# Half tiles for a depthwise convolution, column groups for its norm's sums, and x loaded in pieces

## The reference, cut to what matters

```
u = h @ w_in + b_in                       # h: 2064 x 1024, w_in: 1024 x 3072
a, ga, z = split(u, 3)
glu = a * sigmoid(ga)
c = conv(glu, w_dw) + b_dw                # depthwise over time, 31 taps, causal
c = silu(layer_norm(c, norm_g, norm_b))   # over the 1024 channels
y = (c * silu(z)) @ w_out + b_out
h = layer_norm(ALPHA * h + y, g, b)
```

## Time and profile before

| | us |
|---|---|
| median of three runs (2564.4 to 2571.88) | 2570.7 |
| the profiled execution, its own time | 2562.57 |
| its span on the core | 2560.8 |
| TensorE busy | 2403.9 (94%) |
| VectorE busy | 1304.0 (51%) |
| ScalarE busy | 1099.3 (43%) |
| GpSimd busy | 847.4 (33%) |
| DMA, all queues | 134.50 MB, mean 53 GB/s |

### The profile page before, as it was taken

One profiled execution on the slowest core, in us unless ns is written; L12 is line 12 of the kernel. 1 busy time (PEld: TensorE's weight loads), 2 busy tenths in 40 slices (PEclk: granted clock), 3 DMA queues, 4 the chain that ended last, 5 costly groups with the idle time before them and its releaser, 6 DMA issues. The chain is left out here.

```text
span 2560.8 us, 33174 instructions
## 1 busy us (share of the span) xinstructions
PE 2403.9 (94%) x12822; PEld 1256.0 (49%) x12822; DVE 1304.0 (51%) x2013; ACT 1099.3 (43%) x2060; POOL 847.4 (33%) x592
## 2 busy tenths in 40 slices
PE   7999999868999799999999998997999997999898
PEld 3555555443444355555555554443655554443343
DVE  3898888987553333434334334776145443243422
ACT  5665555345663333434334334334255554222211
POOL 0788777555887101010101010442033332000000
PEclk9999999988999899999999999998999998999899
DMA  5011111032324100100100003223300000100332
GB/s 192 25 42 42 42 42 37 14 132 69 108 99 164 62 1 5 50 1 5 42 1 13 1 1 124 91 87 108 71 9 18 9 1 21 33 1 1 139 105 91
DMA packets 49853, 134.50 MB, mean 53 GB/s; under 512 B 5088, under 2 KB 19040, under 8 KB 48681
## 3 DMA queue, kind: packets, MB, share of 16 engines
q1 hardware_dynamic: 49704, 132.47, 15.5%
HBM read 96.65 MB, written 35.80 MB: 52 GB/s over the span
## 5 line engine op out<-in xcount | busy, mean ns | idle before, releaser
L390 DVE SCALAR_TENSOR_TENSOR cm_tap_sum<-cm_glu,cm_prm,cm_tap_sum 128x2048 f32<-128x2048 f32 x168 | 395.5, 2354 | 49.2 <-ACT cm_tap_sum L248 44.5
L317 POOL TENSOR_TENSOR mixed<-mixed,cm_tap_products 128x2048 f32<-128x2048 f32 x71 | 325.7, 4587 | 88.8 <-ACT cm_tap_products L269 72.7
L91 PE MATMUL cm_proj<-H_hi,cm_w_ga_hi 128*128 128x416 f16 (+1 forms) x640 | 217.8, 340 | 21.9 <-DVE H_lo L364 18.6
L92 PE MATMUL cm_proj<-H_lo,cm_w_ga_hi 128*128 128x416 f16 (+1 forms) x640 | 217.9, 340 | 0.0
L93 PE MATMUL cm_proj<-H_hi,cm_w_ga_lo 128*128 128x416 f16 (+1 forms) x640 | 217.7, 340 | 0.0
L91 PE MATMUL gm_vr<-gm_wvr_hi,H_hi 128*128 128x512 f16 (+1 forms) x544 | 202.8, 373 | 0.0
L93 PE MATMUL gm_vr<-gm_wvr_hi,H_lo 128*128 128x512 f16 (+1 forms) x544 | 202.8, 373 | 0.0
L92 PE MATMUL gm_vr<-gm_wvr_lo,H_hi 128*128 128x512 f16 (+1 forms) x544 | 202.8, 373 | 0.0
L1408 POOL TENSOR_TENSOR gm_q_inter<-gm_q_rel,gm_block_decays 128x512 f32<-128x512 f32 x16 | 16.8, 1047 | 467.0 <-ACT gm_block_decays L1487 467.0
L1943 POOL TENSOR_TENSOR at_probs<-at_probs,at_rsum 128x768 f32<-128x768 f32 (+1 forms) x64 | 90.4, 1412 | 179.1 <-DVE at_rsum L2186 178.9
L1762 DVE SCALAR_TENSOR_TENSOR gm_v_r<-gm_vr,gm_v_r 128x256 f32<-128x256 f32 x64 | 27.1, 424 | 236.9 <-ACT gm_v_r L1506 236.9
(11 more groups left out here) (361 smaller groups left out, 5583.2 us busy)
## 6 DMA issues: line engine op xcount, KB each, us to landing
cm_w_stage<-conv_w SPq DMA_DIRECT2D x24, 512.0 KB, 3.8
co_rows<-x_rows SPq DMA_DIRECT2D x16, 512.0 KB, 4.4
h_rows<-co_rows SPq DMA_DIRECT2D x16, 512.0 KB, 2.9
mixed<-gla_w SPq DMA_DIRECT2D x8, 1024.0 KB, 7.1
go_rows<-h_rows SPq DMA_DIRECT2D x16, 512.0 KB, 4.0
h_rows<-go_rows SPq DMA_DIRECT2D x16, 512.0 KB, 2.8
fo_rows<-h_rows SPq DMA_DIRECT2D x16, 512.0 KB, 3.6
out<-fo_rows SPq DMA_DIRECT2D x16, 512.0 KB, 2.6
```

The costliest lines, as they stand in the source:

```text
L91: nc.tensor.matmul(out, w_hi, x_hi, start=first, stop=False)
L92: nc.tensor.matmul(out, w_hi, x_lo, start=False, stop=False)
L317: nc.gpsimd.tensor_tensor(c_tile(j), c_tile(j), prod[:, r % 2, :], ALU.add).then_inc(s_add, 1)
L390: nc.vector.scalar_tensor_tensor(out=acc[:, :], in0=window(j, k), scalar=col(j, k), in1=acc[:, :], op0=ALU.mult, op1=ALU.add).then_inc(s_t ...
```

## The change

**conv_mix.** A tile is worked on in two halves of 1024 columns, 16 units U. Each half has its own half of the PSUM sum. A first half can start once three of the five token tiles have their glu. The first six units (channel tiles 0 to 2) have 8 products and 21 taps as before; the ten others have 9 products and 20 taps. The products have three slots of 1024 columns. VectorE's taps are no longer given in shares per tile but by `taps_due`. x comes in four pieces per token tile, each with its own semaphore, and the first sections wait piece by piece. The first three weight pieces are scaled inside the halving. `first_tokens` is made in four parts of two channel tiles, one per round 4 to 7.

**conv_out.** Each sum's 8 matmuls have a 128x32 matrix and write to four different 32-partition groups of the bank (k modulo 4), two in each. ScalarE copies both sums to SBUF, and one matmul each with a 128x128 matrix adds the four groups (`totals`), inside the next row. All 8 squares have their own room. The stages of groups 2, 3 and 4 move: totals, mean square and `finish` one row later, `NORMS` one row later, `UNITS` of group 2 in rows 2 to 4 as 3, 3, 2. SyncE's wait before row 3 goes; the ones matrix is set by VectorE.

```diff
@@ conv_mix: counts, schedules, ScalarE and, last, VectorE
-        ACT_TAPS, SUM_TAPS = 1, 9
-        BEFORE = (2, 4, 5, 5, 5)
+        HALF = SEQ // 2
+        UNITS = 2 * KT
-        prod = m.sb("tap_products", [P, 2, SEQ])
+        prod = m.sb("tap_products", [P, 3, HALF])
+        XP = 4
+        def n_products(U):
+            return 8 if U < 6 else 9
+        def taps_before(U):
+            return sum(TAPS - 2 - n_products(V) for V in range(U))
+        def taps_due(j, t):
+            if j < 2:
+                early = max(0, 2 + 6 * (NTT * j + t - 3))
+            else:
+                early = 45 + 9 * (NTT * (j - 2) + t)
+            U, more = ((2 * j - 1, 5), (2 * j - 1, 14), (2 * j - 1, 18), (2 * j, 7), (2 * j, 16))[t]
+            return min(early, taps_before(U) + more if U >= 0 else 0)
...
                 def load_x(t):
+                    for q in range(XP):
+                        sp.dma_start(x_piece(xs, t, q), x_piece(xT.rearrange("(k p) n -> p k n", p=P), t, q)).then_inc(s_x[t][q], 16)
...
+                def start_sum(U):
+                    act.wait_ge(s_glu, U // 2 * NTT + (NTT if U % 2 else 3))
+                    if U >= 2:
+                        act.wait_ge(s_ring, sum_slot(U - 2) + 1)
+                def products(U, first, last):
+                    for i in range(first, last + 1):
+                        r = slot(U, i)
+                        if r >= 3:
+                            act.wait_ge(s_add, r - 2)
+                        nc.scalar.activation(prod[:, r % 3, :], window(U, i), ACT.Copy, scale=col(U // 2, i)).then_inc(s_ring, 1)
+                def read_sum(U):
+                    r = sum_slot(U)
+                    act.wait_ge(s_tap, taps_before(U + 1))
+                    act.wait_ge(s_add, r - 2)
...
+                for j in range(KT):
+                    U = 2 * j
                     for t in range(NTT):
+                        if j and t == 0:
+                            if j >= 2:
+                                read_sum(U - 3)
+                            start_sum(U - 1)
+                            start_c(U - 1)
+                        gate(j, t)
+                        if j and t == 0:
+                            products(U - 2, 7, n_products(U - 2))
+                            products(U - 1, 1, 1)
+                        elif j and t == 1:
+                            products(U - 1, 2, 5)
+                        elif t == 2:
+                            if j:
+                                products(U - 1, 6, 6)
+                                read_sum(U - 2)
+                            start_sum(U)
+                            start_c(U)
+                            if j:
+                                products(U - 1, 7, n_products(U - 1))
+                        elif t == 3:
+                            products(U, 1, 3)
+                        elif t == 4:
+                            products(U, 4, 6)
...
+                for j in range(KT):
+                        taps(done, taps_due(j, t))
+                        done = max(done, taps_due(j, t))
+                        if j >= KT // 2 and t == 2:
+                            first_tokens(j - KT // 2)
+                        gated(j, t)
+                taps(done, taps_before(UNITS))
@@ conv_out
+        TOTALS = {s + 1: T for s, T in STATS.items()}
+        NORMS = {0: (1, range(KT)), 2: (2, range(4)), 3: (2, range(4, 8)), 5: (3, range(4)), 6: (3, range(4, 8)),
+                 9: (4, range(4)), 10: (4, range(4, 8))}
+        UNITS = {0: (1, range(KT)), 2: (2, range(3)), 3: (2, range(3, 6)), 4: (2, range(6, 8))}
+        CG = 4
+        def of_group(ap, k):
+            return ap[k % CG * (P // CG):(k % CG + 1) * (P // CG), :]
+                def group_sums(T):
...
                     for k in range(KT):
-                        nc.tensor.matmul(mean(T), ones[:, :], c_tile(T, k), start=(k == 0), stop=(k == KT - 1))
+                        mm = nc.tensor.matmul(of_group(mean(T), k), ones[:, :], c_tile(T, k), start=(k < CG), stop=(k >= CG))
...
+                def totals(T):
+                    pe.wait_ge(c_cp, 2 * T + 2)
+                    nc.tensor.matmul(mean(T), total[:, :], part[:, 0, 0:w], start=True, stop=True).then_inc(c_e2, 1)
+                    nc.tensor.matmul(spread_of(T), total[:, :], part[:, 1, 0:w], start=True, stop=True).then_inc(c_e2, 1)
```

More of the change, by code:

```diff
@@ L300, in _ @@
+                        if t == (0 if j else 2):
+                            split_w(j, Z)
+                        elif t - 1 in ((0, 1) if j else (2, 3)) and j + 1 < KT:
+                            split_w(j + 1, t - 1 if j else t - 3)
                         if j >= LAG:
                             silu_z(j - LAG, t)
+                read_sum(UNITS - 3)
+                start_sum(UNITS - 1)
+                start_c(UNITS - 1)
+                silu_z(KT - 2, 0)
+                products(UNITS - 2, 7, n_products(UNITS - 2))
@@ new lines, in _ @@
+                silu_z(KT - 2, 1)
+                read_sum(UNITS - 2)
+                products(UNITS - 1, 1, 1)
+                silu_z(KT - 2, 2)
+                products(UNITS - 1, 2, 3)
+                silu_z(KT - 2, 3)
+                products(UNITS - 1, 4, 5)
+                silu_z(KT - 2, 4)
+                products(UNITS - 1, 6, 7)
+                silu_z(KT - 1, 0)
+                products(UNITS - 1, 8, n_products(UNITS - 1))
+                for t in range(1, NTT):
+                    silu_z(KT - 1, t)
@@ L308, in keep_first, with add, add_products, add_sum @@
                     nc.gpsimd.tensor_copy(first[:, j, :], glu[:, j % 2, 0:HALO + META]).then_inc(s_first, 1)
-                def add(j, i):
-                    r = ring_before(j) + i
-                    if i == 0:
-                        pool.wait_ge(s_base, j + 1)
-                    else:
+                def add(U, r):
+                    if slot(U, 1) == r:
+                        pool.wait_ge(s_base, U + 1)
+                    if r:
                         pool.wait_ge(s_add, r)
                     pool.wait_ge(s_ring, r + 1)
-                    nc.gpsimd.tensor_tensor(c_tile(j), c_tile(j), prod[:, r % 2, :], ALU.add).then_inc(s_add, 1)
+                    nc.gpsimd.tensor_tensor(c_unit(U), c_unit(U), prod[:, r % 3, :], ALU.add).then_inc(s_add, 1)
+                def add_products(U, first, last):
+                    for i in range(first, last + 1):
+                        add(U, slot(U, i))
+                def add_sum(U):
+                    add(U, sum_slot(U))
                 def split_w(j, s):
@@ L380, in gated, with taps @@
                         in1=sig[:, i % 2, 0:w], op0=ALU.add, op1=ALU.mult).then_inc(s_glu, 1)
-                def taps(j, first_tap, n):
-                    for i in range(first_tap, first_tap + n):
+                def taps(first, last):
+                    for n in range(first, last):
+                        U = max(V for V in range(UNITS) if taps_before(V) <= n)
+                        i = n - taps_before(U)
                         if i == 0:
-                            dve.wait_ge(s_init, j + 1)
+                            dve.wait_ge(s_init, U + 1)
@@ L418, in _ @@
                 dve.wait_ge(s_ps, 3)
-                for j in range(KT + 1):
-                    done = 0
+                done = 0
+                for j in range(KT):
                     for t in range(NTT):
@@ L554, in conv_out @@
         ident = m.sb("ident", [P, P])
-        ones = m.sb("ones_over_d", [P, P])
+        ones = m.sb("ones_over_d", [P, P // CG])
+        total = m.sb("sum_of_groups", [P, P])
         prm = m.sb("norm_prm", [P, 2 * KT])
-        sq = m.sb("c_squares", [P, 2, GROUP])
+        part = m.sb("group_sums", [P, 2, GROUP])
         sl = m.sb("silu", [P, R, GROUP])
@@ L787, in _ @@
                     if s in STATS:
-                        square(STATS[s], 0)
-                        square(STATS[s], 1)
+                        squares(STATS[s], range(KT))
+                    if s in TOTALS:
+                        mean_square(TOTALS[s])
                     if s >= 2:
@@ L836, in transposes @@
                         mm.then_inc(s_tr, 1)
-                stats(0)
-                stats(1)
+                group_sums(0)
+                totals(0)
+                group_sums(1)
+                totals(1)
                 for s in range(NS + 2):
@@ L855, in _ @@
                             mm.then_inc(s_mm, 1)
+                            if s in TOTALS and h == 0:
+                                totals(TOTALS[s])
                     if s == 2:
@@ L892, in normed @@
                     scaled(ks[-1])
+                nc.vector.memset(ones[:, :], 1.0 / D).then_inc(s_ones, 1)
+                nc.vector.memset(total[:, :], CG / P).then_inc(s_ones, 1)
                 for i, e in enumerate((LN_EPS / ALPHA ** 2, LN_EPS)):
```

276 lines of the change are left out of this document (132 added, 144 removed).

## The result

The changed kernel takes 2536.9 us (median of 4 runs, 2535.0 to 2538.3), the kernel before beside it 2570.0 (4 runs): a ratio of 0.9874, 95% interval 0.9857 to 0.9892. It is faster, by a little over half of what I forecast. The profiled execution spans 2535.4 us, 25.4 less than the one of before.

| stretch | before | after | measured | forecast |
|---|---|---|---|---|
| conv_mix | 559.0 | 526.6 | -32.4 | -36 |
| start of conv_out, to row 1 | 64.0 | 59.9 | -4.1 | -8 |
| rows 1 to 12 | 163.5 | 161.8 | -1.7 | -13.5 |
| row 13 to the gate stage's first product | 62.1 | 64.7 | +2.6 | 0 |
| gate stage to the bias product of attention | 934.6 | 934.9 | +0.3 | 0 |

What follows compares the result with a forecast made beforehand. It took TensorE, with VectorE's waits and tail, to bound conv_mix, and TensorE, with GpSimd next, conv_out. 36 + 8 + 13.5 = 57.5 from 2562.6 gave 2505; with 2513 from the median it took 2509, range 2494 to 2537.

Steps and rivals of the forecast that it cites:

- conv_mix, 36 us forecast: conv_mix: the stage, with its last VectorE add at 520, ends near 523 us instead of 559.
- four banks give it 12 us of room, so I count nothing for it: conv_mix: ScalarE's `gate` stands behind products waiting for slots; counted as 0, or 0 to 8 us without the room.
- the 48 us of GpSimd's work in 42: conv_mix, round 1: GpSimd has 18 adds and three weight halves, 48.4 us in 42; round 2 takes the 6 back.
- the sign that I had named for being wrong: GpSimd as releaser of TensorE's waits, named beside a conv_mix end past 535 us.
- my second rival: GpSimd's ring sets the pace, ScalarE held behind full slots, row 5 later: 8 + 6 us, 2523 in all; 14%.
- the 4 us that I gave for the lower clock and late pieces: conv_mix start: allowance added to the first matmul at 7.7 and 501 us of matmuls, so TensorE alone ends at 513.
- Start of conv_out, 8 us forecast: conv_out before row 1: row 1 starts 56 us into the stage instead of 64.
- About 2.8 us earlier through the chain to `normed` of group 1: Start of conv_out: group 0's sums and squares no longer alternate on cold TensorE, moving group 2's sums from 47.5 to 44.7.
- Rows 1 to 12, 13.5 us forecast: conv_out: row 13 starts 150 us after row 1 instead of 163.5.
- From row 5 on a step is 11.2 for TensorE and 4.85 + 7.05 = 11.9 for GpSimd; over eight steps 95 for both: conv_out from row 5, put at +54 us: both engines need 95 us for eight steps, so row 13 starts at +150.
- After it nothing changes.: From row 13 of conv_out to the kernel's end: no time gained or lost, 0 us.
- taps of 1.54 us: Slower case, conv_mix: a larger fixed part of each of 326 half taps brings the kernel to 2583 us; 4%.

Runs made afterwards that it cites:

- e4: Changed kernel with ScalarE's halving of the round 1 weights put ahead of its products of the first round: 2529.4 us, ratio 0.9849.
- e5: Changed kernel with ScalarE's squares of groups 2 to 4 put ahead of its mean squares of group 1 or gated units: 2527.3 us, ratio 0.9813.
- e6: Changed kernel with conv_out's bias addition moved from GpSimd to VectorE: 2522.3 us, ratio 0.9803.
- e7: Changed kernel with squares first, totals in the same row as the group sums, norms and units placed as in the kernel before: 2523.9 us, ratio 0.9811.
- e8: Changed kernel with the edits of e4, e5, e6 and e7 together: 2512.7 us, ratio 0.9766.

## Why the prediction was wrong

- **conv_mix, 36 us forecast, 32.4 measured.** Right in its terms: first matmul 8.1 (7.7), first tap 44.6 (42.5), a half tap 1.318 (24 in 31.6 us; 1.321), last `gated` 481.7 (483.5), tail over at 518.6 and 1.2 for the last add (520), end 526.6 (523). What failed is the sentence "four banks give it 12 us of room, so I count nothing for it". I had named the 48 us of GpSimd's work in 42 and looked for the harm in ScalarE's `gate`; it came by ScalarE's half of the next weights, behind products that wait for slots. The first section after it starts 7.3 us late, released by GpSimd, the sign that I had named for being wrong. It is near my second rival (ScalarE in order behind full slots), with the size I gave it for this stage (8 us), but at other work and for another reason: e4 takes it away by order alone, and GpSimd's speed is not the bound. That the stage misses by 3.6 and not by 7.3 is in part luck: of the 4 us that I gave for the lower clock and late pieces about 2.4 were used (264 matmuls in 48.35 us, 45.96 at 0.174 each).
- **Start of conv_out, 8 us forecast, 4.1 measured.** "About 2.8 us earlier through the chain to `normed` of group 1" failed: group 2's sums start 48.2 us into the stage, not at 44.7, and its squares end at 58.5, not at 55.4. I took ScalarE's order for given; with the squares ahead (e5) row 1 starts at 52.0, which is more than I forecast. Row 0 starts at 32.6, for 30.8 before, with 17.0 us of waiting for GpSimd's gated units: TensorE was done with all sums by 16 us, and what row 0 waits for is not the sums but the norms and units of group 0. A wait had been filled with matmuls, and taking these out left the wait.
- **Rows 1 to 12, 13.5 us forecast, 1.7 measured.** The largest error. A sum costs 1.9 us (I took 1.8), so the price was right. What failed is "From row 5 on a step is 11.2 for TensorE and 4.85 + 7.05 = 11.9 for GpSimd; over eight steps 95 for both", which lets both run without a gap. Row 5 starts 57.5 us behind row 1, for my 54, and row 13 another 104.3 behind it, for my 96. GpSimd takes its 11.8 us a row, but it stands still four times for 3.0 to 4.6 us, for silus whose norms come late. The squares of groups 3 and 4 were late as well (waits of 3.3 and 1.1 us, and then ScalarE's pace), which I had not counted; but e5 takes these waits away and shortens the stretch by 0.9 only. e6 shortens it by 4.5, norms and units a row earlier (e7 against e5) by 7.9, all together (e8) by 10.5. So the chain to the norms and GpSimd behind it were the bound, and the cheaper sums were hidden by them.
- **"After it nothing changes."** Row 13 takes 12.9 us behind its 4.7 us wait, for 10.5, most of the 2.6: the granted clock is 0.50 for its first 4.8 us. And attention lost 10.2 us: 8.6 without instructions and 1.6 at a clock of 0.83 behind it. No row of before could give that size; the sign of it was there, TensorE waiting 1.3 us for nothing shown in the first `at_p_q`. These 10.2 are in part the choice of executions, as said above.

The misses are 3.6, 3.9, 11.8, 2.6 and 10.2 us, 32.1 in all, which is the distance from 57.5 to 25.4. Two slips in the prediction change none of this: 0.88 us is a third over 0.66 and not a fifth, and taps of 1.54 us add 71 us, which from 2505 gives 2576 and not 2583.

## What to carry to other kernels

When an operation becomes four times cheaper, look at once at what it had hidden: here its own input, the squares, and behind it a chain over three engines that had never been the bound alone. An engine that makes work for two others in program order should make first what the bound engine needs next, and last what waits for a slot. And compare the whole span after a change: a stage far behind it can lose time. Profile more than one execution of each kernel before such a loss is put down to the change.

## What the runs showed of the hardware

- Sixteen fp32 matmuls of 512 columns took 1.92 us in four column groups of 32 and 7.03 us at full width, 3.7 times as long.
- TensorE stood still for 8.6 to 9.0 us with no semaphore to wait for, during a transfer from eight partitions that used under half of the DMA engines' time. The start moved by 32 and 44 matmuls when 64 and 88 idle instructions were put in more than 1200 us earlier, and the end lay 2.3 to 2.5 us behind a 16 KB piece of the instruction queue.
- Eight rows copied 128 times (2 MB) took 44 us out of eight partitions with the eight rows outermost (47% of the DMA engines' time), and 10 us from memory with the 128 copies outermost. Source and order were changed together, so which of them counts is not shown.
